# A fused two-block transformer kernel: expert queries of heads 4 to 7 moved in between the expert slots

## The reference

```python
def peer_ffn(x, w_query, sub_keys, expert_down, expert_up):
    ...
        q = (xc @ w_query).reshape(C, PEER_HEADS, 2, PEER_HALF)
        sc = jnp.einsum('thpd,hpnd->thpn', q, sub_keys).astype(jnp.float32)
        top_s, top_i = lax.top_k(sc, PEER_TOPK)
        cand_s = (top_s[:, :, 0, :, None] + top_s[:, :, 1, None, :]).reshape(...)
        cand_i = (top_i[:, :, 0, :, None] * PEER_NKEYS + top_i[:, :, 1, None, :]).reshape(...)
        best_s, best_pos = lax.top_k(cand_s, PEER_TOPK)
        experts = jnp.take_along_axis(cand_i, best_pos, axis=-1)
        gates = jax.nn.softmax(best_s, axis=-1)
        u = expert_down[experts]
        vv = expert_up[experts]
        act = jax.nn.gelu(jnp.einsum('cd,chkd->chk', xc, u), approximate=False)
        w = (gates * act).astype(xc.dtype)
        return jnp.einsum('chk,chkd->cd', w, vv)
```

## Time and profile before

| | |
|---|---|
| time, median of 3 runs | 1457.46 us (1456.71 to 1459.84) |
| the profiled execution: its time, its span | 1455.62 us, 1453.8 us |
| PE busy | 1247.0 us, 86% |
| DVE, ACT, POOL busy | 810.9, 597.0, 899.0 us |
| HBM read | 396.5 MB, of which the gathers 268.45 MB |
| mean granted TensorE clock | 0.941 of full speed |
| share of the chain that ended last | PE 26%, issue 21%, POOL 18%, DVE 16%, DMA 16% |

### The profile page before, as it was taken

How to read it: one execution, slowest core, us unless ns; L and a number is a source line. 1 busy time by engine, 2 the same in 40 slices (tenths; PEclk the granted TensorE clock), 3 DMA queues, 4 the chain that set the end, 5 groups by cost and what they waited for, 6 DMA issues and landing times.

```text
span 1453.8 us, 17345 instructions
## 1 busy us (share of the span) xinstructions
PE 1247.0 (86%) x5876; PEld 884.7 (61%) x5876; DVE 810.9 (56%) x1518; ACT 597.0 (41%) x1250; POOL 899.0 (62%) x541
## 2 busy tenths in 40 slices
PE   7989797689875878887777788899999989999997
PEld 6768687335332333333333333689999968899886
DVE  5776244766579776667677745432353552269401
ACT  5456353423432322233233222346554444555432
POOL 6963577653545545445544442496869765699985
PEclk9999899899997998889998899999999999999999
DMA  7543448799999999999999998364645643455653
GB/s 269 149 140 118 140 138 347 298 421 394 415 420 420 419 421 419 421 420 420 420 421 419 421 420 333 110 198 138 187 146 160 218 143 116 138 173 190 197 188 101
DMA packets 72942, 400.68 MB, mean 276 GB/s; under 512 B 8096, under 2 KB 8352, under 8 KB 39712
## 3 DMA queue, kind: packets, MB, share of 16 engines
q0 software_dynamic: 36864, 268.45, 44.7%
q1 hardware_dynamic: 33696, 123.35, 26.7%
q10 hardware_dynamic: 2304, 7.85, 1.5%
HBM read 396.48 MB, written 3.15 MB: 275 GB/s over the span
## 4 chain that ended last, share of the span: by engine, by line
PE 26%; issue 21%; POOL 18%; DVE 16%; DMA 16%; ACT 2%; POOLq 0%; ACTq 0%; DVEq 0%
POOL w_lo L1194 16%; DMA arena<-in_experts,arena 12%; PE bank L720 9%; PE bank L531 6%; PE bank L532 5%; PE bank L533 5%; DVE arena L1525 5%; DMA late_rows<-in_experts,arena 4%; DVE arena L1473 1%; DVE arena L1477 1%; DVE arena L1475 1%; POOL stat L1168 1%; DVE arena L1476 1%; DVE arena L1472 1%; POOL arena L1242 1%
## 5 line engine op out<-in xcount | busy, mean ns | idle before, releaser
L1194 POOL TENSOR_TENSOR w_lo<-ring,w_hi 128x1024 fp32r<-128x1024 f32 x222 | 561.9, 2554 | 163.9 <-ACT w_hi L870 163.3
L720 PE MATMUL bank<-arena,diag 128*128 128x512 f32 x896 | 436.8, 646 | 116.8 <-ACT diag L1046 115.2
L1242 POOL DMA_INDIRECT arena<-in_experts,arena x224 | 259.4, 1158 | 285.7 <-PE bank L720 234.6
L720 PEld LDWEIGHTS bank<-arena,diag 128*128 128x128 f32 x896 | 182.2, 207 | 366.8 <-issue 231.4
L1525 DVE CUSTOM_DVE_ANT_0 arena<-arena 128x1024 f32<-128x1024 f32 x224 | 277.6, 1265 | 161.8 <-DMA arena<-in_experts,arena 160.5
L870 ACT ACTIVATE w_hi<-ring 128x1024 fp32r<-128x1024 f32 x228 | 240.6, 1059 | 215.5 <-PE bank L533 171.4
L531 PE MATMUL bank<-hT_hi,w_hi 128*128 128x256 f32 x736 | 209.4, 285 | 4.2 <-DVE hT_lo L1277 2.7
L532 PE MATMUL bank<-hT_lo,w_hi 128*128 128x256 f32 x736 | 208.2, 283 | 0.0
L533 PE MATMUL bank<-hT_hi,w_lo 128*128 128x256 f32 x736 | 208.2, 283 | 0.0
L1037 ACT ACTIVATE arena<-arena 128x4 f32<-128x4 f32 (+1 forms) x66 | 13.5, 205 | 440.2 <-DVE arena L1525 440.2
L531 PEld LDWEIGHTS bank<-hT_hi,w_hi 128*128 128x128 f32 x736 | 141.2, 192 | 5.4 <-issue 5.1
(11 more groups left out here) (231 smaller groups left out, 1777.7 us busy)
## 6 DMA issues: line engine op xcount, KB each, us to landing
ring<-in_stream SPq DMA_DIRECT2D x228, 512.0 KB, 3.5
arena<-in_experts,arena POOLq DMA_INDIRECT x224, 16.9
kv_park<-arena ACTq DMA_DIRECT2D x8, 256.0 KB, 4.3
arena<-kv_park ACTq DMA_DIRECT2D x1, 2048.0 KB, 9.0
x_res<-in_x SPq DMA_DIRECT2D x2, 512.0 KB, 5.5
arena<-in_mem SPq DMA_DIRECT2D x1, 1024.0 KB, 11.5
arena<-in_sub_keys ACTq DMA_DIRECT2D x1, 1024.0 KB, 4.9
out<-arena SPq DMA_DIRECT2D x2, 512.0 KB, 2.6
```

What stands on the lines that cost most here:

```text
L720: mm = pe.matmul(y_banks[half][:, :], diag[:, slot % DIAGS, :], rows_buf[BUFFER[slot]][:, D + 512 * half:D + 512 * half + 512], start=(i = ...
L1194: nc.gpsimd.tensor_tensor(w_lo[:, slot, :], ring[:, slot, :], w_hi[:, slot, :].bitcast(F32), ALU.subtract).then_inc(S("lo_made"), 1)
L1242: nc.gpsimd.indirect_dma_start(out=rows_buf[b], out_offset=None, in_=experts, in_offset=bass.IndirectOffsetOnAxis(ap=expert_u[:, slot:slot ...
```

## The change

Heads 0 to 3 are queried ahead of the slots, in the order of `QUERY_ORDER`, with the scores of head 0 directly behind its queries. The chunks of heads 4 to 7 are worked on between slots (`CHUNK_AT`: slots 3 and 7 of units 0 to 3), their scores at slot 11 of the same unit (`SUB_AT`); then come the four chunks of xv1 one by one, at slots 64, 68, 72 and 76. POOL makes their low parts two slots ahead in its own order (`LOW_AT`), ACT the high parts ten slots ahead (`HI_AT`). Since queries and sub-keys live longer, only 8 buffers are used up to slot 71, 11 up to slot 96, and 13 from slot 97 on. ACT weighs in batches of two up to slot 95, then of four. `select` is cut into four parts, at slots 5, 8, 11 and 14 of a unit. The scaled activations are made behind the first two `select`s. The sums of the two tiles keep PSUM banks 4 to 7 over the whole stage, with a semaphore of their own (`y_done`); queries, scores and xv1 take turns on banks 0 to 3. POOL works out the norm of the first tile one low part after the last chunk of w_out instead of four.

```diff
-LAST_BATCHES = [(SLOTS - 4, 2), (SLOTS - 2, 1), (SLOTS - 1, 1)]
-FIRST_LO = 10
-FIRST_GATHERS = 8
-BUFFER = [s % 11 if s < 55 else (s - 44) % GATHERS for s in range(SLOTS)]
+AHEAD_HEADS = 4
+CHUNK_AT = [16 * (h - AHEAD_HEADS) + at for h in range(AHEAD_HEADS, PEER_H) for at in (3, 7)]
+SUB_AT = {16 * (h - AHEAD_HEADS) + 11: h for h in range(AHEAD_HEADS, PEER_H)}
+CHUNK_AT += [CHUNK_AT[-1] + 9 + 4 * i for i in range(4)]
+VALUES_AT = CHUNK_AT[-4]
+HI_AT = {at - 10: i for i, at in enumerate(CHUNK_AT) if at >= 10}
+LOW_AT = {max(at - 2, 8): i for i, at in enumerate(CHUNK_AT)}
+FEW, MORE = 72, 97
+FIRST_LO = 8
+PARTS_AT = [5, 8, 11, 14]
+BUFFER = [s % 8 if s < FEW else (s - FEW + 8) % 11 if s < MORE else (s - MORE + 11) % GATHERS for s in range(SLOTS)]
+BATCHES = [(slot, 2) for slot in range(0, MORE - 1, 2)] + [(slot, BATCH) for slot in range(MORE - 1, SLOTS - 4, BATCH)]
+BATCHES += [(SLOTS - 4, 2), (SLOTS - 2, 1), (SLOTS - 1, 1)]
+QUERY_ORDER = [("query", 0), ("sub", 0), ("query", 1), ("query", 2), ("sub", 1), ("query", 3), ("sub", 2), ("sub", 3)]
...
+        if key[0] == "y":
+            bank = 4 + 2 * key[1] + key[2]
+        else:
+            bank = turn % (4 if key[0] in ("query", "sub") or key[:2] == ("xv", 1) else 8)
+            turn = bank + 1
...
                     if slot == VALUES_AT:
-                        natural("xv", 4, 1, h_, FIRST["xv1"] - 4)
+                        xv_banks = [open_bank(pe, ("xv", 1, tile)) for tile in range(TT)]
+                    if slot in CHUNK_AT:
+                        i_chunk = CHUNK_AT.index(slot)
+                        h, j = AHEAD_HEADS + i_chunk // 2, i_chunk % 2
+                        if h >= PEER_H:
+                            value_chunk(i_chunk - 2 * (PEER_H - AHEAD_HEADS), xv_banks)
+                        else:
...
+                    if slot in SUB_AT:
+                        sub_scores(SUB_AT[slot])
...
+            for first, count in BATCHES:
+                weigh(first, count)
+                for slot in range(first, first + count):
+                    u, k = slot // PEER_K, slot % PEER_K
+                    if slot in HI_AT:
+                        hi_parts(FIRST["query"] + 2 * AHEAD_HEADS + HI_AT[slot])
+                    if slot - 2 in CHUNK_AT[1:2 * (PEER_H - AHEAD_HEADS):2]:
+                        query_out(AHEAD_HEADS + CHUNK_AT.index(slot - 2) // 2)
+                    if slot - 2 in SUB_AT:
+                        sub_out(SUB_AT[slot - 2])
...
-            norm("ffn")
+            lo_parts(LAST["w_out"] + 1)
+            norm_tile("ffn", 0)
+            lo_parts(LAST["w_out"] + 3)
+            norm_tile("ffn", 1)
             lo_parts(FIRST["query"] + FIRST_LO - 1)
...
             for slot in range(SLOTS):
-                if slot == FIRST_GATHERS:
-                    lo_parts(LAST["query"] + RING)
+                if slot in LOW_AT:
+                    lo_parts(FIRST["query"] + 2 * AHEAD_HEADS + LOW_AT[slot])
...
                 for k in range(PEER_K):
-                    if k == PEER_K // 2 and u + 2 < UNITS:
-                        select(u + 2)
+                    if k in PARTS_AT and u + 2 < UNITS:
+                        select(u + 2, PARTS_AT.index(k))
```

More of the change, by code:

```diff
@@ L213, in plan @@
     natural("mlp_down", 2, 16, FIRST["mlp_down"])
-    table, results, last = {}, 0, -1
-    for n, (key, chunk) in enumerate(order):
+    table, results, last, turn, uses = {}, 0, -1, 0, [0] * 8
+    for key, chunk in order:
         last = chunk if chunk is not None else last
-        results += chunk is None
-        table[key] = (n, chunk, results, last)
+        results += chunk is None and key[0] != "y"
+        if key[0] == "y":
[3 more added lines that the diff above has]
+            turn = bank + 1
+        table[key] = ((bank, uses[bank]), chunk, results, last)
+        uses[bank] += 1
     return table
@@ L702, in sub_scores, with value_chunk @@
                 mm.then_inc(result_done, 1)
-            for h in range(PEER_H + 1):
-                if h < PEER_H:
+            for kind, h in QUERY_ORDER:
+                if kind == "query":
                     transposed("query", h, normed("ffn") if h == 0 else None, h_1)
-                if h > 0:
-                    sub_scores(h - 1)
+                else:
+                    sub_scores(h)
+            def value_chunk(i, xv_banks):
+                wait_weight(FIRST["xv1"] + i)
+                for tile in range(TT):
+                    for kk in range(2):
+                        k = 2 * i + kk
+                        mm = product(xv_banks[tile][:, :], [part[:, tile * P:(tile + 1) * P] for part in hT[k]],
+                                     weight(FIRST["xv1"] + i, slice(kk * 512, (kk + 1) * 512)), k == 0, k == KT - 1)
+                mm.then_inc(chunk_done, 1)
             for t in range(TT):
@@ L876, in hi_before @@
                 last = at[key][3]
-                hi_parts(last + RING - 1 if last >= 0 else 1)
+                ahead = last + RING - 1 if last >= 0 else 1
+                hi_parts(min(ahead, FIRST["query"] + 2 * AHEAD_HEADS - 1) if key[0] in ("query", "sub") else ahead)
             def copy_out(key, dst, scale=1.0, n=512, last=True, src=None):
@@ L1542, in _ @@
             for u in range(2):
-                select(u)
-            for u in range(2):
-                finish_gates(u)
+                for part in range(4):
+                    select(u, part)
+            dve.wait_ge(S("gain_loaded"), 16)
+            for t in range(TT):
+                dve.wait_ge(S("rstd"), 2 * seq["ffn"] + t + 1)
+                own.mark(v.scalar_tensor_tensor(xn[:, t, :], xs[:, t, :], rstd["ffn"][:, t:t + 1], gain_rows,
+                                                ALU.mult, ALU.mult))
+            own.sync()
             for u in range(UNITS):
                 for k in range(PEER_K):
-                    if k == PEER_K // 2 and u + 2 < UNITS:
-                        select(u + 2)
-                    if k == PEER_K // 2 and u == PEER_H:
+                    slot = u * PEER_K + k
+                    if k in PARTS_AT and u + 2 < UNITS:
+                        select(u + 2, PARTS_AT.index(k))
+                    if k == 8 and u == PEER_H:
                         mix_add(0)
-                    dot(u * PEER_K + k)
-                if u + 2 < UNITS:
-                    finish_gates(u + 2)
-                if u == PEER_H + 1:
-                    mix_scale(0)
+                    if k == 10 and u == PEER_H + 1:
+                        mix_scale(0)
+                    if slot == 2:
+                        finish_gates(0)
+                    if k == (13 if u == 0 else 3) and u + 1 < UNITS:
+                        finish_gates(u + 1)
+                    dot(slot)
             mix_add(1)
```

159 lines of the change are left out of this document (78 added, 81 removed).

## The result

The changed kernel took 1446.03 us (median; 1442.94 to 1447.93) beside 1458.65 us (1456.71 to 1460.11) for the kernel before, four runs each: a ratio of 0.9914 with a 95% interval of 0.9898 to 0.9931. The forecast was 1446.1. A second series on another occasion gave 1441.27 us (1440.29 to 1441.95, 4 runs) beside 1457.16 (9 runs), ratio 0.9888 [0.9872, 0.9904]. So the gain is 12.6 us by the first series and 15.9 by the second. The mechanism is in the main the forecast one; one step of it failed, F, and is told further down.

A forecast was written before the change was run, and what follows sets the result against it. The expert slots were taken as bound by the DMAs' rate; -6.4 (A) -10.5 (B) +2.5 (C) +3.0 (D) +0 (E) = -11.4 us from 1457.5 gave 1446.1; own range 1441.5 to 1452, 8 in 10 up to 1455.

The forecast's parts named there:

- F: Batches of two, last batches, PSUM banks and xv1 chunks no longer in one block: claimed to cost and win nothing.
- A: Start of the expert slots: first gather comes 6.4 us earlier, at 220.0 instead of 226.4; bounds 3 and 6.6.
- The scores' part: Start: scores of head 0 directly behind its queries begin 4.6 us earlier, and so does the select.
- The part from locks: Inside the first select: a tiny step held 2.13 us beside POOL's low parts becomes free; 1.8 us taken as gained.
- B: Behind the first eight gathers: the DMA hole at 255 to 290 us goes, winning 10.5 us.
- C: Weight loads: two more 512 KB loads fall into the stage, costing 2.5 us (1.3 if one already did).
- D: New hole at the stage's start, DMAs dry before gather 8 and in the first slots: costs 3 us, 0 to 6.
- E: Eight buffers for slots 8 to 71: 5.9 us spare per 20.0 us turn, so cost 0, up to 4 us.
- The sum of 14.1: Time in us a buffer needs per turn: bytes, fixed latency 4.2 at most, batch partner, dot, weights, PE slot, POOL.
- Rivals 1 and 2: Eight buffers now and then too few, 1454 us (0.13); low parts between gathers hold the pipeline, 1462 us (0.07).
- Rival 3: Slots with eight buffers: DMAs slower with few gathers outstanding, 381 GB/s costing 18 us, 1464 us; chance 0.06.
- One or two windows below 400, none below 300: Expected sign: DMA rate in GB/s in 5 us windows between 240 and 275 us, at the stage's start.

The follow-up runs named there:

- start_alone: Kernel before with only its start changed (earlier head 0 scores, activations behind selects, norms' order, eight low parts ahead of gathers): 1458.49 us, ratio 1.0002.
- extra_loads: Changed kernel plus eight unread 512 KB HBM-to-HBM copies, one every eight slots from slot 143 to 199: 1454.04 us, ratio 0.9971 to before.

## Why the prediction was right, and where it was not

*A, 6.4 us.* Measured 27.66 - 20.96 = 6.7. The scores' part is 4.5 (4.6 predicted). The part from locks is 2.2 (1.8 taken), and its reason is half right: the tiny step of the earlier trace rows is free now (0.17), but another step is held for 2.04. Before, a second step had been held too, a TENSOR_TENSOR (L1488) of 2.67 us for 0.42 of work. One hold of two went. And A is no term by itself, as start_alone shows.

*B, 10.5 us.* Gone, as said (10.7 by the table).

*C, 2.5 us.* 14 loads before, 16 now, at the price that extra_loads measured: 2.2 to 2.5.

*D, 3 us, 0 to 6.* It was 5.0 in the first profile and 2.0 in the second. I had let a low part hold the second of the two activations, until 236 (T0 + 16); in the first profile both low parts held the last step of the select, and both activations came behind, to T0 + 17.2. ACT's batch took 1.5 instead of 1.1. That is gather 8 at T0 + 25.7 instead of 24.0, so D was sized 2 us too small for this execution. The other courses, with the low parts behind the activations, I did not foresee. The first slots ran at PE's lower level (granted clock 0.50 in the windows from 235 to 245), as taken.

*E, 0.* The window from 290 to 890 has 420 GB/s. That some 6 us are spare is borne out from the other side: seven buffers take 2.5 of them and cost a few us, six take 5.0 and cost 25. The sum of 14.1 itself was about 0.8 too large, since the latency is 3.4 to 3.6 in the rows above and not 4.2. Rivals 1 and 2 (the spare time is gone) did not come; with six buffers, or with batches of four, it is gone, and the kernel loses 17 to 29 us. Rival 3 (slower DMAs with few gathers outstanding) is out.

*F, nothing.* This is the step of the forecast that failed. "That block let POOL wait 10.73 us, under full DMAs, so nothing is won": the DMAs were full at 350 but ran dry at 360, and 2.9 us went there. I had read the average of the earlier trace rows, which begins at 400, for a stretch that lies ahead of it. The line of 40 slices shows it too: the slice from 327 to 363 us has 394 GB/s, so the full rate holds from about 370 on and not from 330, as the section on time and profile before says. No run tests F alone; its 2.9 us are read from these windows. The four low parts, now at slot 112, are under full DMAs as said, though a dot is held 9.83 us by them.

The balance from q0 to the last dot, first profile: 6.7 (A) + 10.7 - 5.0 (B, D) + 3.0 - 0.4 (F) - 2.3 (C) = 12.7; read 708.1 - 696.7 = 11.4. Second profile: 15.6; read 14.2. Some 1.3 us are not accounted for in either. That the forecast of 1446.1 met 1446.0 is luck in its last us: F's 2.9 us were missing on one side, and on the other D was 2 short and that rest unknown. With F in it the sum is 14.3 and the time 1443.2, between the two series.

*What would show it.* The first gather at 222.5 instead of 220, because q0 was 2.8 us later in that execution, in work that the change leaves as it was (in others q0 lay between 197.3 and 202.5). "One or two windows below 400, none below 300" was wrong in detail: four, and one at 252. The granted clock from 290 to 890 was 0.92, beside 0.89 before. The last dot was at 898.3, 895.5 without that shift.

## What to carry to other kernels

When a stage runs at the rate of the DMAs, look for every window in which they don't, over the whole stage and not in one average: the holes, and the bytes themselves, are all there is to win. An earlier start won nothing here while the next thing that holds the pipeline stayed where it was. Fewer buffers are free only while a buffer's turn has room for the disturbances that meet in it, and small batches and cut-up blocks on the engines made that room here. A gain of a few us in four runs wants the two kernels side by side again before it is believed.
